# The last three v blocks of a PEER layer, tile by tile, with the norm of each tile behind it

## The chip, the core and the metric

The kernel runs on one core of a Trainium2 chip. The metric is the time of the whole program on the device in microseconds (us), lower is better: 3424.29 us for the kernel before, the median of three runs that gave 3423.9, 3424.29 and 3427.24. A core has a matmul engine (TensorE, called PE in the profile, with its weight loads as PEld), a vector engine (DVE), an activation engine (ACT), GpSimd (POOL), and a queue that issues DMAs (SP). Each engine works through its own instructions in order and waits on semaphores for the others.

## The reference, cut to what matters

The input is 512 tokens of width 1024. There are two residual layers. Each mixes tokens by attention, adds the result to the residual stream `x`, and then adds PEER, a layer of 16384 experts of which every token takes 16 for each of 8 heads:

```python
def rmsnorm(x, g):
    y = xf * lax.rsqrt(jnp.mean(xf * xf, axis=-1, keepdims=True) + NORM_EPS)
    return y * g

    def chunk(args):                       # one chunk of PEER
        h = jax.nn.gelu(jnp.einsum('cd,chkd->chk', xc, u[ec]), approximate=False)
        return jnp.einsum('chk,chkd->cd', gc * h, v[ec])

    for l in range(DEPTH):                 # DEPTH is 2
        ...
        x = x + jnp.concatenate([mix, mo], axis=-1) @ w_out[l]
        x = x + peer(rmsnorm(x, norm_ffn[l]), ...)
        if l == N_A_LAYERS - 1:            # after the first layer
            kv = (rmsnorm(x, shared_norm) @ shared_w_kv)...
    return rmsnorm(x, final_norm)
```

What matters here comes after each PEER: after the first layer the sum of squares of every row of `x`, its root and the normed and turned `x` (features on partitions) for the projections of the second layer; after the second layer the same norm, times the final gain, as the output.

## The kernel before

`x` is kept in SBUF as four tiles of 128 tokens by 1024 features. The program is a row of stages. Each stage has its own buffers and semaphores and ends with a barrier over all engines, so nothing of a later stage starts before the last instruction of the one before has ended.

`peer_stage` (once for each layer) walks over 272 blocks of 128 by 1024 weights: 16 of the query projection, 128 of u, 128 of v. ACT rounds a block to its high part (`hi`, a ring of three), DVE or POOL takes the low part (`lo`), and PE multiplies in three passes: high by high, high by low, low by high. The v blocks multiply the gated hiddens of token tiles 1 to 3, held as `w_hi` and `w_lo` in chunks of four blocks, and add up in six PSUM banks `bank[:, t, half, :]`, where t is 0 to 2 for tiles 1 to 3 and half is one of two halves of 512 features. Token tile 0 is done otherwise: DVE takes its experts' rows one by one and adds them in `acc`. SP loads the blocks, each when the low part four blocks earlier is done.

In `values(n)` PE does all 18 products of one v block and goes to the next. So all six banks are complete only with the last block. Then DVE adds the two `acc` halves to tile 0 (this part comes earlier, while PE works) and adds the banks to tiles 1 to 3, and the stage ends.

After the first layer the stage `turn_stage` ("sht") squares and sums every tile (two on ACT, two on DVE), takes one root for all four, writes four 128 by 128 matrices `diag` with the reciprocal roots on their diagonal, and for each of 8 feature blocks lets PE multiply the four tiles' columns by them, which scales and turns `x` at once. ACT copies the high part out of PSUM and DVE subtracts it for the low part. `value_stage` ("sv") then begins with its weights' DMA. Beside this, SP brings the memory keys and values into SBUF. After the second layer `rstd_stage` ("fin") does all four sums of squares on DVE, and `final_stage` multiplies by the reciprocal root and the gain and stores the tiles.

`out_stage`, earlier in each layer, is not touched. It already works on `x` tile by tile (sum of a half, Square of a half, root, `diag`, turn), with the same kinds of instruction that the change adds, and its functions are cited as "o_" rows.

Of the kernel before, what the change touches and what calls it, by code (L numbers as in the profile page):

```python
# [18 lines left out]
F32 = mybir.dt.float32  # L19
# [67 lines left out]
class Side:  # L87

    def __init__(self, st, pairs):  # L90
        self.pairs = pairs
        self.loaded = [st.sem(f"side{n}") for n in range(len(pairs))]

    def start(self, sp):
        for (dst, src), sem in zip(self.pairs, self.loaded):
            sp.dma_start(dst, src).then_inc(sem, 16)

    def wait(self, sp):
        for sem in self.loaded:
            sp.wait_ge(sem, 16)  # L100

# [25 lines left out]

def rstd_stage(nc, name, src, width, out, side=()):  # L130

    n_src = len(src)
    with Stage(nc, name) as st:
        junk = st.sb("junk", [P, width])
        ssq = st.sb("ssq", [P, n_src])
        squared, meaned, rooted, done = [st.sem(s) for s in ("squared", "meaned", "rooted", "done")]
        side = Side(st, side)
        with nc.Block() as block:
            @block.sync
            def _(sp):  # L140
                side.start(sp)
                side.wait(sp)

            @block.vector
            def _(dve):
                for n in range(n_src):
                    if n:

                        dve.wait_ge(squared, n)
                    dve.tensor_tensor_reduce(junk[:, :], src[n], src[n], 1.0, 0.0, ALU.mult, ALU.add,  # L150
                                             ssq[:, n:n + 1]).then_inc(squared, 1)
                dve.wait_ge(squared, n_src)
                dve.tensor_scalar(ssq[:, :], ssq[:, :], 1.0 / width, EPS, ALU.mult, ALU.add).then_inc(meaned, 1)
                dve.wait_ge(rooted, 1)
                dve.reciprocal(out, ssq[:, :]).then_inc(done, 1)
                dve.wait_ge(done, 1)

            @block.scalar
            def _(act):
                act.wait_ge(meaned, 1)  # L160
                act.activation(ssq[:, :], ssq[:, :], ACT.Sqrt).then_inc(rooted, 1)

def turn_stage(nc, name, ident, parts, out, gain, rstd=None, norm=True, side=()):

    out_hi, out_lo = out
# [2303 lines left out]
```

## Time and profile before

| What | Value |
|---|---|
| Time, median of three runs | 3424.29 us |
| Time of the profiled execution | 3423.7 us |
| Its span (first to last instruction) | 3421.9 us |
| Mean granted PE clock | 0.977 of full speed |
| PE busy | 3255.3 us (95%) |
| DVE busy | 2667.6 us (78%) |
| ACT busy | 1400.2 us (41%) |

### The profile page before, as it was taken

What the parts mean: (1) busy time and instruction counts of PE and PEld (TensorE: products, weight loads), DVE (VectorE), ACT (ScalarE), POOL (GpSimd) and SP (SyncE); (2) the same over time, 40 slices, a digit from 0 to 9 for tenths busy, and PEclk for the clock granted to TensorE, in tenths of its full rate; (3) what the DMA queues carried; (4) which work ended last, traced back from release to release, by engine and by line L of the source; (5) the groups of instructions that cost most, each with busy time, mean ns of one, the idle gap of its engine ahead of it and who ended that gap; (6) DMA issues with size and microseconds to landing.
All of it is one profiled execution on the core that took longest, in us unless ns stands there. A gap on an engine that the chain in (4) does not pass through costs nothing. (4 is left out here: it accounts for less than half of the span.)

```text
span 3421.9 us, 49213 instructions
## 1 busy us (share of the span) xinstructions
PE 3255.3 (95%) x18534; PEld 2913.3 (85%) x18534; DVE 2667.6 (78%) x5415; ACT 1400.2 (41%) x2205; POOL 1098.5 (32%) x666
## 2 busy tenths in 40 slices
PE   7988999999999999998999997999999999999997
PEld 6866899999998888886978876899989998888886
DVE  4664799888976889885367875799898976888886
ACT  3333245544453333333345544235545453333332
POOL 1311363333422465550000001354242422455451
PEclk9998999999999999999999999999999999999999
DMA  4102358878889999994122212348778789999994
GB/s 164 62 7 89 127 163 288 297 268 294 274 310 352 406 392 402 387 397 144 71 80 69 75 44 81 130 138 293 288 268 282 271 313 350 409 398 394 392 396 178
DMA packets 324348, 833.65 MB, mean 244 GB/s; under 512 B 26000, under 2 KB 160656, under 8 KB 320016
## 3 DMA queue, kind: packets, MB, share of 16 engines
q1 hardware_dynamic: 250384, 562.04, 45.8%
q0 software_dynamic: 73728, 268.47, 21.3%
q8 instruction: 148, 2.42, 0.3%
q14 instruction: 88, 0.72, 0.1%
HBM read 721.30 MB, written 109.10 MB: 243 GB/s over the span
## 5 line engine op out<-in xcount | busy, mean ns | idle before, releaser
L1959 ACT ACTIVATE peer_hi<-peer_raw 128x1024 fp32r<-128x1024 f32 x540 | 570.7, 1057 | 648.8 <-PE p_bank L1933 501.1
L2173 DVE TENSOR_TENSOR peer_lo<-peer_raw,peer_hi 128x1024 fp32r<-128x1024 f32 x434 | 532.0, 1226 | 315.2 <-ACT peer_hi L1959 314.9
L1862 POOL DMA_INDIRECT p_grow<-in_u_rows,p_expert x256 | 331.2, 1294 | 750.1 <-DVE p_hid L2181 736.1
L1862 POOL DMA_INDIRECT p_grow<-in_v_rows,p_expert x256 | 425.1, 1660 | 372.4 <-DVE p_acc L2190 331.4
L1933 PE MATMUL p_bank<-peer_hi,p_w_hi 128*128 128x512 f32 x1536 | 473.1, 389 | 0.8 <-DVE peer_lo L2173 0.8
L1933 PE MATMUL p_bank<-peer_hi,p_w_lo 128*128 128x512 f32 x1536 | 473.0, 389 | 0.0
L1933 PE MATMUL p_bank<-peer_lo,p_w_hi 128*128 128x512 f32 x1536 | 472.8, 389 | 0.0
L1884 PE MATMUL p0r_h_ps<-peer_x_hi,peer_hi 128*128 128x384 f32 (+1 forms) x1152 | 400.8, 348 | 9.7 <-ACT p_h_sb L1973 5.8
L1884 PE MATMUL p1r_h_ps<-peer_x_hi,peer_hi 128*128 128x384 f32 (+1 forms) x1152 | 401.1, 348 | 9.3 <-ACT p_h_sb L1973 5.6
L1884 PE MATMUL p1r_h_ps<-peer_x_hi,peer_lo 128*128 128x384 f32 (+1 forms) x1152 | 394.9, 343 | 0.0
L1884 PE MATMUL p1r_h_ps<-peer_x_lo,peer_hi 128*128 128x384 f32 (+1 forms) x1152 | 394.9, 343 | 0.0
L1884 PE MATMUL p0r_h_ps<-peer_x_hi,peer_lo 128*128 128x384 f32 (+1 forms) x1152 | 394.8, 343 | 0.0
L1884 PE MATMUL p0r_h_ps<-peer_x_lo,peer_hi 128*128 128x384 f32 (+1 forms) x1152 | 394.7, 343 | 0.0
L1850 POOL TENSOR_TENSOR peer_lo<-peer_raw,peer_hi 128x1024 fp32r<-128x1024 f32 x106 | 267.9, 2529 | 372.7 <-ACT peer_hi L1959 372.1
L1933 PEld LDWEIGHTS p_bank<-peer_hi,p_w_hi 128*128 128x128 f32 x1536 | 288.1, 188 | 61.4 <-DVE peer_lo L2173 1.7
L1933 PEld LDWEIGHTS p_bank<-peer_hi,p_w_lo 128*128 128x128 f32 x1536 | 288.3, 188 | 60.0
L1933 PEld LDWEIGHTS p_bank<-peer_lo,p_w_hi 128*128 128x128 f32 x1536 | 288.3, 188 | 59.8
L2181 DVE CUSTOM_DVE_ANT_0 p_grow<-p_grow,p_xrow 128x1024 f32<-128x1024 f32 x256 | 318.2, 1248 | 0.8
L2190 DVE SCALAR_TENSOR_TENSOR p_acc<-p_grow,p_w,p_acc 128x1024 f32<-128x1024 f32 x252 | 317.6, 1279 | 0.0
L1884 PEld LDWEIGHTS p0r_h_ps<-peer_x_hi,peer_hi 128*128 128x128 f32 x1152 | 218.5, 190 | 15.3 <-issue 9.1
L1884 PEld LDWEIGHTS p1r_h_ps<-peer_x_hi,peer_hi 128*128 128x128 f32 x1152 | 218.6, 190 | 15.0 <-issue 8.6
L1884 PEld LDWEIGHTS p1r_h_ps<-peer_x_lo,peer_hi 128*128 128x128 f32 x1152 | 218.3, 189 | 5.2
(365 smaller groups left out, 5589.2 us busy)
## 6 DMA issues: line engine op xcount, KB each, us to landing
peer_raw<-in_u SPq DMA_DIRECT2D x256, 512.0 KB, 5.0
peer_raw<-in_v SPq DMA_DIRECT2D x256, 512.0 KB, 9.1
hiddens<-p_h_sb SPq DMA_DIRECT2D x256, 192.0 KB, 3.7
p_w_raw<-hiddens SPq DMA_DIRECT2D x64, 768.0 KB, 8.0
p_g_sb<-gates SPq DMA_DIRECT2D x64, 768.0 KB, 11.7
gates<-x SPq DMA_DIRECT2D x12, 2048.0 KB, 9.6
ba_w<-in_w_b_mix SPq DMA_DIRECT2D x38, 512.0 KB, 3.6
peer_raw<-in_w_peer_q SPq DMA_DIRECT2D x32, 512.0 KB, 3.8
```

Source lines behind the costliest of these rows:

```text
L1850: pool.tensor_tensor(lo[:, m % NH, :], raw[:, m % NR, :], hi[:, m % NH, :].bitcast(F32), ALU.subtract).then_inc(lo_pool, 1)
L1862: pool.indirect_dma_start(out=grow[:, g % RG, :], out_offset=None, in_=table, in_offset=bass.IndirectOffsetOnAxis(ap=expert[:, at:at + 1], ...
L1884: mm = pe.matmul(h_ps[:, n % 2, first:S], a[:, n % NH, at], b[:, k, first:S], start=(k == 0 and s == 0), stop=(k == KC - 1 and s == 2))
L1933: mm = pe.matmul(bank[:, t, half, :], w[:, c % 2, b, t * P:(t + 1) * P], v[:, n % NH, half * HALF:(half + 1) * HALF], start=j == 0 and s = ...
L1959: act.activation(hi[:, n % NH, :], raw[:, n % NR, :], ACT.Copy).then_inc(hi_ready, 1)
L2173: dve.tensor_tensor(lo[:, m % NH, :], raw[:, m % NR, :], hi[:, m % NH, :].bitcast(F32), ALU.subtract).then_inc(lo_dve, 1)
L2181: dve.tensor_tensor_reduce(row, row, xrow[:, :], 1.0, 0.0, ALU.mult, ALU.add, hid0[:, at:at + 1]).then_inc(used, 1)
L2190: dve.scalar_tensor_tensor(out=acc[:, at % 2, :], in0=row, scalar=w0[:, at:at + 1], in1=acc[:, at % 2, :], op0=ALU.mult, op1=ALU.add).then ...
```

## The change

- **v blocks.** The first 125 v blocks go as before. For the last three (`GROUP0` onwards) PE goes over tile and half first and over the blocks inside: nine products for tile 1's first half, nine for its second half, and so on. A half is complete after its nine. The number of products is the same.
- **Tails.** The sum, the norm and the turn (first layer) or the final scaling and the store (second layer) are in `peer_stage`, tile by tile: tile 0, whose sum needs no PE, then 1, 2, 3. ACT does all the Squares, by halves of 512. `turn_x(0)` stands behind the nine products (0,1), `turn_x(1)` behind (2,0), and `turn_x(2)` and `turn_x(3)` behind the last.
- **Stages.** `turn_stage`, `rstd_stage` and `final_stage` are gone. The memory keys and values are loaded in `dilated_stage`, behind its first two weight tiles. The final gain is loaded into `xrow` 40 blocks into the v blocks. The output is stored from `x`.
- **Buffers.** The pair of normed and turned `x` (`h_hi`, `h_lo`) is one buffer for the whole program, where each part had its own.

```diff
@@ peer_stage, SP
+                    if n == FRONT + 40 and final is not None:
+                        sp.wait_ge(used, PAIRS)
+                        sp.dma_start(xrow[:, :], final[0]).then_inc(final_loaded, 16)
+                if final is not None:
+                    for t in range(TT):
+                        sp.wait_ge(scaled, t + 1)
+                        sp.dma_start(final[1][tokens(t), :], x[:, t, :]).then_inc(y_stored[t], 16)
...
@@ peer_stage, PE
-                for n in range(FRONT, BLOCKS):
+                def last_values(t, c, n):
+                    j = n - FRONT
+                    if t == 0 and c == 0:
+                        wait_lo(pe, n)
+                    for s, (w, v) in enumerate(((w_hi, hi), (w_hi, lo), (w_lo, hi))):
+                        mm = pe.matmul(bank[:, t, c, :], w[:, j // CH % 2, j % CH, tokens(t)], v[:, n % NH, half(c)],
+                                       start=False, stop=j == NK - 1 and s == 2)
+                    if n == BLOCKS - 1:
+                        mm.then_inc(halves_done, 1)
+
+                def turn_x(t):
+                    pe.wait_ge(diag_ready, t + 1)
...
+                    for f in range(KC):
+                        if t and f % 4 == 0:
+
+                            pe.wait_ge(x_lo_ready, 2 * (t - 1) + f // 4 + 1)
+                        mm = pe.matmul(turn_ps[:, f // 4, (f % 4) * P:(f % 4 + 1) * P], x[:, t, f * P:(f + 1) * P],
+                                       diag[:, t, :], start=True, stop=True)
+                        if f % 4 == 3:
+                            mm.then_inc(x_turned, 1)
+
+                for n in range(FRONT, GROUP0):
                     values(n)
...
+                for t in range(TD):
+                    for c in range(2):
+                        for n in range(GROUP0, BLOCKS):
+                            last_values(t, c, n)
+                        if final is None and (t, c) in ((0, 1), (2, 0)):
+                            turn_x(t // 2)
+                if final is None:
+                    turn_x(2)
+                    turn_x(3)
@@ peer_stage, ACT
+                for t in range(TT):
+                    for c in range(2):
+                        act.wait_ge(added, x_half_done(t, c))
...
+                        act.activation(junk[:, half(c)], x[:, t, half(c)], ACT.Square,
+                                       accum_out=ssq[:, t, c:c + 1]).then_inc(x_squared, 1)
+                    act.wait_ge(x_meaned, t + 1)
+                    act.activation(ssq[:, t, 1:2], ssq[:, t, 1:2], ACT.Sqrt).then_inc(x_rooted, 1)
+                    if final is None:
+                        for b in range(2):
+                            act.wait_ge(x_turned, 2 * t + b + 1)
+                            act.activation(x_hi[:, 4 * b:4 * b + 4, tokens(t)],
+                                           turn_ps[:, b, :].rearrange("p (f j) -> p f j", j=P),
+                                           ACT.Copy).then_inc(x_hi_ready, 1)
@@ peer_stage, DVE
-                dve.wait_ge(summed, BLOCKS)
-                for t in range(TD):
-                    to = x[:, t + 1, :]
-                    dve.tensor_tensor(to, bank[:, t, :, :].rearrange("p a b -> p (a b)"), to,
-                                      ALU.add).then_inc(added, 1)
-                dve.wait_ge(added, TD + 2)
+                for t in range(TT):
+                    if t:
+                        for c in range(2):
+                            dve.wait_ge(halves_done, 2 * (t - 1) + c + 1)
+                            to = x[:, t, half(c)]
+                            dve.tensor_tensor(to, bank[:, t - 1, c, :], to, ALU.add).then_inc(added, 1)
...
+                    if final is not None:
+                        dve.scalar_tensor_tensor(out=x[:, t, :], in0=x[:, t, :], scalar=rstd[:, t:t + 1],
+                                                 in1=xrow[:, :], op0=ALU.mult, op1=ALU.mult).then_inc(scaled, 1)
+                        continue
+                    dve.tensor_scalar(diag[:, t, :], ident[:, :], rstd[:, t:t + 1], None,
+                                      ALU.mult).then_inc(diag_ready, 1)
+                    for b in range(2):
+                        dve.wait_ge(x_hi_ready, 2 * t + b + 1)
...
@@ dilated_stage, SP
                 load(0)
                 load(1)
+                sp.dma_start(mem_kT[:, :, :], mem_dram[:, 0, :, :]).then_inc(mem_k_loaded, 16)
+                sp.dma_start(mem_v[:, :, :], mem_dram[:, 1, :, :]).then_inc(mem_v_loaded, 16)
```

The two places of which the prediction speaks follow, as the instructions stand in the built programs. The first is DVE at the end of the first layer's PEER. `x<-p_acc,x` is the sum of tile 0, `x<-p_bank,x` that of tiles 1 to 3, `sht_` names belong to the stage that is removed. Before:

```order
L2173 TENSOR_TENSOR peer_lo<-peer_raw,peer_hi 128x1024 x3
L2253 TENSOR_TENSOR x<-p_acc,x 128x1024 x2
L2257 TENSOR_TENSOR x<-p_bank,x 128x1024 x3
L1799 UNCONDITIONAL_BRANCH
L231 UNCONDITIONAL_BRANCH
L239 ISA sht_junk,sht_ssq<-x 128x1024
L239 ISA sht_ssq 128x1
```

And now, to the first row of tile 2:

```order
L2119 TENSOR_TENSOR peer_lo<-peer_raw,peer_hi 128x1024 x3
L2199 TENSOR_TENSOR x<-p_acc,x 128x1024 x2
L2209 TENSOR_SCALAR p_ssq<-p_ssq 128x1
L2213 SCALAR_TENSOR_TENSOR p_ssq<-p_ssq 128x1
L2216 RECIPROCAL rstd<-p_ssq 128x1
L2222 TENSOR_SCALAR p_diag<-ident,rstd 128x128
L2227 TENSOR_TENSOR h_lo<-p_turn_ps,h_hi 128x4x128 x2
L2207 TENSOR_TENSOR x<-p_bank,x 128x512 x2
```

The sum of tile 1 (L2207) stands behind the whole tail of tile 0, and so on for tiles 2 and 3.

The second place is PE at the same time: the end of the nine products (0,1), the turn of tile 0, and the start of the products (1,0). Before, nothing stood between products there.

```order
L1847 MATMUL p_bank<-peer_hi,p_w_hi 128x512
L1847 MATMUL p_bank<-peer_lo,p_w_hi 128x512
L1847 MATMUL p_bank<-peer_hi,p_w_lo 128x512
L1861 MATMUL p_turn_ps<-p_diag,x 128x128 x8
L1847 MATMUL p_bank<-peer_hi,p_w_hi 128x512
L1847 MATMUL p_bank<-peer_lo,p_w_hi 128x512
```

The eight turns have moved from a stage of their own to a place ahead of 36 of the 54 last products.

The third place is DVE at the end of the second layer. There the tail of a tile is the scaling by root and gain:

```order
L2199 TENSOR_TENSOR x<-p_acc,x 128x1024 x2
L2209 TENSOR_SCALAR p_ssq<-p_ssq 128x1
L2213 SCALAR_TENSOR_TENSOR p_ssq<-p_ssq 128x1
L2216 RECIPROCAL rstd<-p_ssq 128x1
L2219 SCALAR_TENSOR_TENSOR x<-x,rstd,p_xrow 128x1024
L2207 TENSOR_TENSOR x<-p_bank,x 128x512 x2
```

The scaling of tile 0, which was the first of four in the last stage, now stands ahead of the sum of tile 1.

## Rows read from the trace of the kernel before

**Rows 1.** The page's first part: busy time and share by engine.

```profile
PE 3255.3 (95%) x18534; PEld 2913.3 (85%) x18534; DVE 2667.6 (78%) x5415; ACT 1400.2 (41%) x2205; POOL 1098.5 (32%) x666
```

**Rows 2.** Windows (start:end, length; PE, PEld, DVE, ACT, POOL; clock; DMA share, GB/s), first boundary.

```profile
1594.00:1602.70 8.70, 0.00 (x0) 0.00 (x0) 6.08 (x11) 3.79 (x6) 0.00 (x0) 0.63 0.19 62
1602.70:1605.00 2.30, 2.28 (x10) 2.28 (x11) 0.56 (x3) 0.17 (x1) 0.00 (x0) 0.50 0.00 0
```

**Rows 3.** Timeline (start, length, engine, line, operation, [idle before]), end of first layer.

```profile
1581.02 0.62 PE L1933 MATMUL p_bank<-peer_hi,p_w_hi 128*128 128x512 f32 x2
1581.28 1.06 ACT L1959 ACTIVATE peer_hi<-peer_raw 128x1024 fp32r<-128x1024 f32 x1 [3.02 <-PE p_bank L1933]
...
1582.37 1.23 DVE L2173 TENSOR_TENSOR peer_lo<-peer_raw,peer_hi 128x1024 fp32r<-128x1024 f32 x1 [2.85 <-ACT peer_hi L1959]
1583.51 2.48 DVE L2253 TENSOR_TENSOR x<-p_acc,x 128x1024 f32<-128x1024 f32 x2
...
1592.80 0.61 PE L1933 MATMUL p_bank<-peer_hi,p_w_lo 128*128 128x512 f32 x2
1593.46 3.49 DVE L2257 TENSOR_TENSOR x<-p_bank,x 128x1024 f32<-128x1024 f32 x3 [7.46 <-PE p_bank L1933]
...
1598.13 1.06 ACT L221 ACTIVATE sht_junk<-x 128x1024 f32<-128x1024 f32 x1 [15.80 <-PEq L126]
...
1612.56 0.69 DVE L252 SCALAR_TENSOR_TENSOR dil_h_lo<-sht_bank,dil_h_hi 128x512 fp32r<-128x512 f32 x1 [0.20 <-ACT dil_h_hi L228]
1614.22 10.55 SPq L282 DMA_DIRECT2D sv_w<-in_w_shared_v  x12
```

**Rows 4.** Timeline, end of second layer and of the program.

```profile
3389.66 0.62 PE L1933 MATMUL p_bank<-peer_hi,p_w_hi 128*128 128x512 f32 x2
...
3392.15 2.48 DVE L2253 TENSOR_TENSOR x<-p_acc,x 128x1024 f32<-128x1024 f32 x2
3402.10 3.49 DVE L2257 TENSOR_TENSOR x<-p_bank,x 128x1024 f32<-128x1024 f32 x3 [7.47 <-PE p_bank L1933]
3406.76 1.28 ACT L161 ACT_TABLE_LOAD   x1 [15.78 <-PEq L126]
3406.84 1.23 DVE L150 CUSTOM_DVE_ANT_0 fin_junk<-x 128x1024 f32<-128x1024 f32 x1 [1.25 <-PEq L126]
...
3413.42 4.88 DVE L2271 SCALAR_TENSOR_TENSOR final_y<-x,rstd,gain_rows 128x1024 f32<-128x1024 f32 x4 [0.89 <-PEq L126]
```

**Rows 5.** Timeline of `out_stage` in the second layer: tile 0, then tile 3.

```profile
2098.96 0.63 ACT L1544 ACTIVATE o_junk<-x 128x512 f32<-128x512 f32 x1 [5.67 <-DVE x L1588]
...
2100.52 1.28 ACT L1547 ACT_TABLE_LOAD   x1
...
2102.25 0.29 DVE L1601 TENSOR_SCALAR o_diag<-ident,rstd 128x128 f32<-128x128 f32 x1
...
2137.07 0.69 DVE L1588 TENSOR_TENSOR x<-o_bank,x 128x512 f32<-128x512 f32 x1 [3.40 <-PE o_bank L1492]
...
2139.60 2.05 PE L1503 MATMUL o_t_ps<-o_diag,x 128*128 128x128 f32 x16 [2.56 <-DVE o_diag L1601]
2140.35 2.18 ACT L1553 ACTIVATE peer_x_hi<-o_t_ps,gains 128x128 fp32r<-128x128 f32 x8 [1.32 <-PE o_t_ps L1503]
```

**Rows 6.** Timeline of `out_stage` in the first layer: the turn of tile 3.

```profile
330.07 3.57 PE L1503 MATMUL o_t_ps<-o_diag,x 128*128 128x128 f32 x16 [2.57 <-DVE o_diag L1601]
```

**Rows 7.** Windows of one microsecond in these two turns.

```profile
330.00:331.00 1.00, 0.93 (x4) 0.93 (x5) 0.02 (x1) 0.00 (x0) 0.00 (x0) 0.50 0.00 0
...
2140.00:2141.00 1.00, 1.00 (x11) 1.00 (x11) 0.00 (x0) 0.65 (x3) 0.00 (x0) 1.00 0.00 0
```

**Rows 8.** Groups by line (count | busy, mean ns | idle before): table loads of the second `out_stage`.

```profile
L1547 ACT ACT_TABLE_LOAD x1 | 1.3, 1283 | 0.0
```

**Rows 9.** Issues of DMAs (queue, count, KB each, median us to landing).

```profile
x<-stream SPq DMA_DIRECT2D x2, 2048.0 KB, 17.2
```

**Rows 10.** Waits of PE (us in total, times, longest) in the second layer's v blocks.

```profile
PE p_bank L1933 <- DVE peer_lo L2173: 0.2, 1, 0.2
```

More of the change, by code:

```diff
@@ L84, in __call__ @@
         self.wait()
[L87 to L100, printed above, removed]
 class Stage:
@@ L127, in __exit__ @@
         self.ctx.close()
[L130 to L161, printed above, removed]
@@ L338, in _, with dilated_stage @@
                         dve.tensor_copy(out(t, c), bank[:, n % 4, 0:cw]).then_inc(moved, 1)
-def dilated_stage(nc, name, ident, ident_b, masks, h, w_dram, gain, rope, v, mem, o, mix_dram):
+def dilated_stage(nc, name, ident, ident_b, masks, h, w_dram, gain, rope, v, mem, mem_dram, o, mix_dram):
     HALF = 2 * P
@@ L1636, with peer_stage @@
 NTD = SD // TB
-def peer_stage(nc, name, ident, iota16, iota2, h, ring, src, x, rstd, rows_of, drams):
+def peer_stage(nc, name, ident, iota16, iota2, h, ring, src, x, rstd, rows_of, drams, final=None):
     BATCH = 8
@@ L2283, in trunk @@
+                if final is None:
+                    dve.wait_ge(x_lo_ready, 2 * TT)
 def trunk(nc, a, out):
@@ L2361, in trunk @@
             with Stage(nc, "dil") as st2:
-                h = pair(st2, "h")
-                turn_stage(nc, "sht", ident, [(x[:, t, :], lambda f: None) for t in range(TT)], h,
-                           lambda f: None, rstd[:, :],
-                           side=[(tile[:, :, :], mem_dram[:, n, :, :]) for n, tile in enumerate(mem)])
                 v = st2.sb("v", [P, TT, NT * P])
@@ L2376, in gain @@
                     return gains[:, which, k:k + 1]
-                dilated_stage(nc, "ba", ident, ident_b, masks, h, a["w_b_mix"], gain, (cos, sin), v, mem, o,
+                dilated_stage(nc, "ba", ident, ident_b, masks, h, a["w_b_mix"], gain, (cos, sin), v, mem, mem_dram, o,
                               mix_dram)
             peer_st = Stage(nc, "peer1")
-            h, ring = peer_buffers(peer_st)
-            mix_out(1, o, True, lambda f: None, h, ring)
-        peer(1, h, ring)
+            ring = peer_ring(peer_st)
+            mix_out(1, o, True, lambda f: None, ring)
+        peer(1, ring, (a["final"].broadcast_to([P, D]), out))
         peer_st.ctx.close()
-        gain_rows = sb("gain_rows", [P, D])
-        rstd_stage(nc, "fin", [x[:, t, :] for t in range(TT)], D, rstd[:, :],
-                   side=[(gain_rows[:, :], a["final"].broadcast_to([P, D]))])
-        final_stage(nc, x, rstd, gain_rows, out)
 def shape_constants():
```

165 lines of the change are left out of this document (56 added, 109 removed).

## The prediction

> **What bounds the kernel now.** I read the page's busy times first: PE is busy 95% of the span [rows 1], so the change, which keeps every product, can only win where PE has nothing to do. Then I took the windows and the timeline around the end of each PEER layer. At the first end PE stands idle for the whole of 1594.00 to 1602.70 and then turns `x` at clock 0.50 [rows 2]. In the timeline the stretch that the change rewrites begins with the first product of the third-last v block, at 1581.02, and ends with the last low part, 1612.56 + 0.69 = 1613.25 [rows 3]. At the second it begins at 3389.66 and ends with the last scaled tile, 3413.42 + 4.88 = 3418.30 [rows 4]. A gain or a loss is a shift of these two ends, 32.2 and 28.6 us after their starts; what follows them (a barrier and the next weights; a store) stays. The reader is to see in the rows which engine ends last in each stretch: DVE, in both.
>
> **Start of the group, same in both layers.** The last v block is rounded by ACT only when the fourth-last is multiplied (1581.28), and its low part is ready at 1582.37 + 1.23 = 1583.60 [rows 3]. Before, PE needed it 36 products later. Now PE needs it after six. A product takes 0.227 us (54 products from 1581.02 to the end of 1592.80 + 0.61, less the overlap of the last) [rows 3], so PE arrives at 1582.38 and waits 1.27 us. Products (0,0) then end at 1584.33 and (0,1) at 1586.37. DVE adds tile 0 at 1583.51 to 1585.99, as before [rows 3].
>
> **Links of a tail.** `out_stage` has run the same chain, so I take its durations [rows 5]. With the table load of the first Sqrt, from the first Square to `diag` is 2102.25 - 2098.96 = 3.29, and PE starts 0.34 later, 3.63 in all. Without it, from the second half's sum to PE is 2139.60 - 2137.07 = 2.53. Two half sums follow each other by about 0.61 (0.69 less an overlap of 0.08; three of 1024 take 3.49 [rows 3]), and the two Squares with their reads are 0.82 apart, which adds 0.21: 3.35 from the first sum to PE. The eight turns take 2.05 at full clock. ACT's copy began 0.75 after the first two of them (0.51 of issue), so 0.24 behind; the second bank's copy is then at 2.29, its low part at about 2.91 to 3.60 after PE's start. The next tile's sum starts 0.07 before that end, so 3.53 after PE's start. Where a tail ends in scaling, it starts where `diag` would (3.01 after the first sum) and takes 1.20 in a row (4.88 for four [rows 4]).
>
> **First layer, at full clock.** Tile 0: Square at 1586.03, PE at 1589.66. PE had nothing since 1586.37, so it stalls 3.3 us in the middle of its products, and 36 products queue behind the waiting turn. Turn to 1591.71, 27 products to 1597.83, then `turn_x(1)`: here DVE is early (sum at 1593.19, `diag` for 1596.5) and PE is the bound. Sum of tile 2 at 1601.36, PE at 1604.71 (its last products ended at 1601.92: idle 2.8). Sum of tile 3 at 1608.24, PE at 1611.59 (idle 4.8), end 1615.19. Before it was 1613.25: **1.9 us later**. The barrier behind it takes 1.18 us at this stage's end (1596.95 to 1598.13) where the removed stage's took 0.97 (1613.25 to 1614.22) [rows 3]: **+0.2**. So in the first layer the overlap costs more than it brings, since DVE runs the tails one after the other and most of them come after the products. The reader can see it in DVE's order: each sum of a bank stands behind the whole tail of the tile ahead.
>
> **Second layer.** No turn, so PE runs through. DVE: Square at 3392.15 + 2.48 + 0.04 = 3394.67, scaling of tile 0 at 3397.96, sum of tile 1 at 3399.16, and then 3.01 + 1.20 = 4.21 for each tile: sums at 3403.37 and 3407.58, last scaling 3410.59 to 3411.87. Before: 3418.30. **6.4 us earlier.** The banks are ready well before (the last about 3403.5). The end of this stage has more semaphores to clear than the final stage had; between nothing and the 0.3 us by which two stage ends already differ I take **+0.2**.
>
> **The clock.** PE's three idle stretches in the first layer (3.3, 2.8, 4.8 us) each stand ahead of a turn. The trace has the same case twice with both outcomes: after 2.57 us of idle one turn ran at clock 0.50 and took 3.57 us, after 2.56 the other at 1.00 and took 2.05 [rows 5 to 7]. So a cold turn costs 1.5 us, and each turn lies on the chain (`turn_x(0)` through PE's queue, 2 and 3 through DVE's). Bounds: 0 and 4.6 for three. The idles here are as long as or longer than the two seen, so I take two of three, **+3.0**.
>
> The Trainium skill speaks against the change here (TensorE: Matmul & The Clock Gate, "HAM oscillation"): bursts of matmuls with waits between them fall back to the low clock and start cold each time. The trace agrees in one of its two cases, at 0.50, and not in the other, at 1.00. By that rule all three turns are cold, which is the second rival below.
>
> **Table load.** Square and Copy cause no load of their own in `out_stage`: one load, of 1.28 us, for four tiles [rows 5, 8]. Before, in the last stage, it lay under DVE's squares (3406.76 [rows 4]); now it is on the chain of tile 0, and is in the 3.29. The skill (ScalarE: Activation LUTs, "What ACT_TABLE_LOAD costs") has some 2.66 us for a switch, with a drain beside the load. By that both layers would end some 1.4 us later, an estimate from that page; the trace shows the root's instruction directly behind the load's 1.28 us, and the sum goes by the trace.
>
> **Cover of what costs nothing.** The gain row (512 KB) joins a stream of loads that fills the DMA engines. The load of `x` in the same blocks is 2048 KB [rows 9], and PE waited 0.2 us in all of the second layer's v blocks [rows 10]: 0, at most 1.3. SP's wait ahead of it is on rows used some 20 blocks earlier. The memory keys and values move behind two weight tiles of `dilated_stage`, and the first scores come two tiles of products later: 0, at most 1. The one home for `h` moves no instruction: 0. The added matmul order in one bank keeps the weight load for each product, as now: 0.
>
> **Sum.** +1.9 + 0.2 - 6.4 + 0.2 + 3.0 = -1.1, on the profiled execution's 3423.7: 3422.6. The median of the runs lies 0.6 above the profiled one (3424.29), so **3423.2 us**.
>
> **Rivals.**
> 1. The clock holds in all three idles. For it: the turn at 2139.60. Against it: the turn at 330.07, with a shorter idle ahead than any here. Then -4.1: 3420.2 us.
> 2. Slower than before: all three turns cold. Place: `turn_x(0)`, `turn_x(2)`, `turn_x(3)` in the first layer. Price 3 x 1.5 = 4.6, and it decides from the point where cold turns cost over 4.1 us, that is, with the third. For it: each idle is over 2.57 us, the last 4.8. Against it: 2139.60. Then +0.5: 3424.8 us; if products near a turn are caught too, some 1.5 more.
> 3. The tails do go under the products. Then only tile 3's tail is exposed: second layer, last half complete at 3403.4, its scaling about 3405.6 to 3406.9, 11.4 saved; first layer, products done at 1600.6, PE 2.5 later, end 1606.8, 6.4 saved. 3406.5 us. Against it: DVE's order, and that the first `diag` needs a chain of over 6 us from the group's start. For it only that PE would be busy all the time in the second layer, which is not where the end is.
> 4. The change does not overlap without cost elsewhere: the gain row holds up the v stream by its full 1.3 us and the memory loads `dilated_stage` by 1. 3425.5 us. The wait of 0.2 us [rows 10] speaks against it.
>
> **How the numbers follow.** Forecast 0.50, rival 1 0.19, rival 2 0.19, rival 3 0.05, rival 4 0.03; the rest, 0.04, is for layouts and stage ends that no row shows, of either sign. What a measurement can tell from no change is about 0.2%, or 6.8 us: faster means below 3417.4, slower above 3431.1. Forecast and rivals 1, 2 and 4 lie inside: same 0.89. Faster is rival 3 and a part of the rest: 0.07. Slower is the rest: 0.04. The range from 3418.8 to 3427.0 holds the first two rivals with the cost bounds of about 1.3 on one side and of 2.3 on the other.
>
> **What would show it.** In the first layer: PE waits for `peer_lo` once, about 1.3 us, in the first group; then for `diag` three times, about 3.3, 2.8 and 4.8 us; the windows at the turns show 0.50 at two of them; the last `h_lo` comes 34 to 39 us after the group's first product, not under 32.2. In the second: scalings 4.2 us apart, the last ending 22.2 us after the group's first product instead of 28.6. The prediction is wrong if the first layer's stretch gets shorter than 32.2 us, if the tails' period is not about 4.2 us, if PE's v blocks lose time elsewhere, or if the table is loaded more than once in a stage's tail.

## The result, and the profile after

The changed kernel takes 3436.11 us (median of 20 runs, 3423.5 to 3440.39), the kernel before, run beside it, 3428.14 us (median of 20, 3422.7 to 3437.19). The ratio is 1.002, with a 95% interval of 1.0013 to 1.0028: slower by 4.5 to 9.6 us. The prediction said 3423.2 us, no change, in a range that ended at 3427.0. It was wrong. (In a later set one run of the kernel before and one of `c1_final_fill` took over 4400 us in a slower state of the chip; the ratios leave both out.)

The profiled execution took 3434.58 us with a span of 3432.8 us, 10.9 us over the span before. First the page: PE is busy 16.2 us longer than before [rows 1], though the trace has the same 18534 matmul records. A busy time that grows with the same work is the first sign of a lower clock.

```profile
PE 3271.5 (95%) x18534; PEld 2922.8 (85%) x18534; DVE 2664.0 (78%) x5429; ACT 1410.7 (41%) x2239; POOL 1087.3 (32%) x666
```

**The first rewritten stretch.** The timeline of the changed kernel at the end of the first layer, which answers to [rows 3]: the group's first product, PE's wait for the last low part, the four turns of `x`, the last low part, the next stage's first load and its first product.

```profile
1581.18 0.39 PE L1847 MATMUL p_bank<-peer_hi,p_w_hi 128*128 128x512 f32 x1
...
1583.68 2.48 DVE L2199 TENSOR_TENSOR x<-p_acc,x 128x1024 f32<-128x1024 f32 x2
...
1583.82 0.50 PE L1847 MATMUL p_bank<-peer_hi,p_w_hi 128*128 128x512 f32 x1 [1.11 <-DVE peer_lo L2119]
...
1589.81 3.55 PE L1861 MATMUL p_turn_ps<-p_diag,x 128*128 128x128 f32 x16 [2.94 <-DVE p_diag L2222]
...
1599.38 1.95 PE L1861 MATMUL p_turn_ps<-p_diag,x 128*128 128x128 f32 x16
...
1605.92 3.16 PE L1861 MATMUL p_turn_ps<-p_diag,x 128*128 128x128 f32 x16 [2.51 <-DVE p_diag L2222]
...
1613.68 3.57 PE L1861 MATMUL p_turn_ps<-p_diag,x 128*128 128x128 f32 x16 [4.60 <-DVE p_diag L2222]
...
1617.91 0.69 DVE L2227 TENSOR_TENSOR h_lo<-p_turn_ps,h_hi 128x512 fp32r<-128x512 f32 x1 [0.80 <-ACT h_hi L1967]
...
1619.88 3.84 SPq L138 DMA_DIRECT2D sv_w<-in_w_shared_v  x8
...
1624.39 0.69 PE L173 MATMUL sv_bank<-sv_w_hi,h_hi 128*128 128x384 f32 x1 [7.14 <-DVE sv_w_lo L181]
```

The stretch lasts from 1581.18 to 1618.60, 37.4 us against 32.2 before [rows 3]: +5.2. The barrier behind it takes 1.28 instead of 0.97: +0.3. The windows inside three of the turns (columns as in [rows 2]) show the clock, where 0.50 is the low level: low in the first and the fourth, low for most of the third, full in the second, which follows 27 products without a wait.

```profile
1590.00:1593.00 3.00, 3.00 (x15) 3.00 (x16) 0.45 (x1) 0.60 (x1) 0.00 (x0) 0.50 0.00 0
1599.50:1601.00 1.50, 1.50 (x16) 1.50 (x15) 0.00 (x0) 0.53 (x1) 0.00 (x0) 1.00 0.00 0
1606.00:1609.00 3.00, 3.00 (x16) 2.79 (x16) 0.69 (x1) 0.60 (x1) 0.00 (x0) 0.61 0.00 0
1614.00:1617.00 3.00, 3.00 (x16) 3.00 (x15) 0.58 (x1) 0.60 (x1) 0.00 (x0) 0.52 0.00 0
```

**The second rewritten stretch.** The end of the program in the changed kernel, which answers to [rows 4]: the group's first product, the table load, the four scalings.

```profile
3406.73 0.39 PE L1847 MATMUL p_bank<-peer_hi,p_w_hi 128*128 128x512 f32 x1
...
3413.30 1.28 ACT L1963 ACT_TABLE_LOAD   x1
...
3415.02 1.28 DVE L2219 SCALAR_TENSOR_TENSOR x<-x,rstd,p_xrow 128x1024 f32<-128x1024 f32 x1
...
3419.22 1.28 DVE L2219 SCALAR_TENSOR_TENSOR x<-x,rstd,p_xrow 128x1024 f32<-128x1024 f32 x1
...
3423.41 1.28 DVE L2219 SCALAR_TENSOR_TENSOR x<-x,rstd,p_xrow 128x1024 f32<-128x1024 f32 x1
...
3427.60 1.28 DVE L2219 SCALAR_TENSOR_TENSOR x<-x,rstd,p_xrow 128x1024 f32<-128x1024 f32 x1
```

It lasts from 3406.73 to 3428.88, 22.15 us against 28.64 [rows 4]: -6.5. From there to the end of the span are 3.9 us against 3.6: +0.3. The two stretches with their ends sum to 5.5 - 6.2 = -0.7 us. The span grew by 10.9. So 11.6 us were lost in stages whose instructions the change does not touch.

**Where they are.** I compared the starts of the same products, stage by stage. The second layer's attention is as long as before up to the last product into `ba_bank` (the query and key projections of `dilated_stage`): the changed kernel gains 0.5 us there. Then come the last attention units of `dilated_stage`, which have no projection between them, and `out_stage`. From the last `ba_bank` product to the first product of the second PEER layer (`p1r_h_ps`) it is 2021.3 to 2144.3 before and 2026.3 to 2162.2 after: 123.0 against 135.9 us, **+12.9**. The second PEER layer up to its rewritten end gives 0.8 back.

Windows over this stretch, its first 50 us and the rest, of the kernel before, and a third up to its last attention unit:

```profile
2021.30:2071.30 50.00, 35.67 (x296) 29.95 (x294) 27.08 (x71) 21.61 (x67) 0.00 (x0) 0.96 0.07 23
2071.30:2144.30 73.00, 59.33 (x289) 49.17 (x289) 36.70 (x70) 33.25 (x72) 9.55 (x4) 0.91 0.25 87
...
2021.30:2067.10 45.80, 35.41 (x296) 29.83 (x294) 23.53 (x60) 21.40 (x66) 0.00 (x0) 1.00 0.08 25
```

and of the changed kernel:

```profile
2026.30:2076.30 50.00, 40.48 (x265) 32.89 (x265) 22.61 (x55) 19.59 (x62) 0.00 (x0) 0.80 0.06 17
2076.30:2162.20 85.90, 66.83 (x322) 55.42 (x321) 41.03 (x86) 35.62 (x78) 9.54 (x4) 0.86 0.22 77
```

In the first 50 us the granted clock is 0.80 instead of 0.96, and PE gets through 265 instructions instead of 296, busy for longer. By these mean clocks PE had the low level for some 44 us of the stretch, against some 17 before. Work that takes 27 us at half the clock takes 13.5 less at full clock, an estimate from the two pairs of rows, and the stretch is 12.9 longer.

The timeline of PE shows how it begins. Before, an attention unit with a wait of 2.40 us for DVE and the one behind it:

```profile
2034.02 1.97 PE L506 MATMUL ba_o_ps<-dil_v,ba_eT 128*128 128x64 f32 x16 [2.40 <-DVE ba_both L649]
...
2035.82 0.59 PE L467 MATMUL ba_s_ps<-masks,ident_b 128*128 128x512 bf16 x2
...
2037.42 1.09 PE L517 MATMUL ba_t_ps<-ident,ba_e 128*128 128x128 f32 x8
...
2039.66 1.97 PE L506 MATMUL ba_o_ps<-dil_v,ba_eT 128*128 128x64 f32 x16 [1.15 <-ACT ba_eT L550]
```

and the same two units in the changed kernel:

```profile
2039.02 2.63 PE L369 MATMUL ba_o_ps<-dil_v,ba_eT 128*128 128x64 f32 x16 [2.39 <-DVE ba_both L512]
...
2041.45 1.06 PE L327 MATMUL ba_s_ps<-masks,ident_b 128*128 128x512 bf16 x2
...
2044.45 1.97 PE L380 MATMUL ba_t_ps<-ident,ba_e 128*128 128x128 f32 x8
...
2047.53 2.00 PE L369 MATMUL ba_o_ps<-dil_v,ba_eT 128*128 128x64 f32 x16 [1.11 <-ACT ba_eT L413]
```

The wait ahead is the same to 0.01 us. Then the same matmuls take 1.06 instead of 0.59 and 1.97 instead of 1.09. The clock did not fall in the wait itself. Windows of the changed kernel, from the wait's end on:

```profile
2039.02:2040.10 1.08, 1.08 (x10) 1.08 (x10) 0.00 (x0) 1.08 (x6) 0.00 (x0) 1.00 0.00 0
2040.10:2047.00 6.90, 6.31 (x30) 4.68 (x29) 1.91 (x4) 0.74 (x3) 0.00 (x0) 0.51 0.01 2
```

PE worked for 1.1 us at the full clock, and then the clock was low for 6.9 us in which PE was busy. In the kernel before it stayed full behind the same wait. The next unit's first product waits for ACT's `ba_eT`, which waits for PE's transposes `ba_t_ps`, so the unit is 2.9 us longer (2039.02 to 2047.53, 8.51 us, against 5.64).

### The profile page after: what moved, and what is told of

Read it like the earlier page. It is cut to its first block and busy times, and to the rows that moved or that the text cites. A ratio compares the mean times of both kernels' runs of the same rounds, so it can differ in the third digit from the quotient of the medians.

```text
span 3432.8 us, 49215 instructions
## 1 busy us (share of the span) xinstructions
PE 3271.5 (95%) x18534; PEld 2922.8 (85%) x18534; DVE 2664.0 (78%) x5429; ACT 1410.7 (41%) x2239; POOL 1087.3 (32%) x666
## 5 line engine op out<-in xcount | busy, mean ns | idle before, releaser
L1756 POOL DMA_INDIRECT p_grow<-in_v_rows,p_expert x256 | 413.6, 1616 | 388.2 <-DVE p_acc L2136 350.2
L1778 PE MATMUL p0r_h_ps<-h_hi,peer_hi 128*128 128x384 f32 (+1 forms) x1152 | 401.1, 348 | 11.3 <-ACT p_h_sb L1903 5.7
L1778 PE MATMUL p1r_h_ps<-h_hi,peer_hi 128*128 128x384 f32 (+1 forms) x1152 | 400.9, 348 | 9.1 <-ACT p_h_sb L1903 5.6
L1778 PE MATMUL p1r_h_ps<-h_hi,peer_lo 128*128 128x384 f32 (+1 forms) x1152 | 394.8, 343 | 0.0
L1778 PE MATMUL p0r_h_ps<-h_lo,peer_hi 128*128 128x384 f32 (+1 forms) x1152 | 394.7, 343 | 0.0
L1778 PE MATMUL p1r_h_ps<-h_lo,peer_hi 128*128 128x384 f32 (+1 forms) x1152 | 394.6, 343 | 0.0
L1778 PE MATMUL p0r_h_ps<-h_hi,peer_lo 128*128 128x384 f32 (+1 forms) x1152 | 394.5, 342 | 0.0
L1778 PEld LDWEIGHTS p0r_h_ps<-h_hi,peer_hi 128*128 128x128 f32 x1152 | 218.4, 190 | 17.4 <-issue 9.2
L1778 PEld LDWEIGHTS p1r_h_ps<-h_hi,peer_hi 128*128 128x128 f32 x1152 | 218.5, 190 | 14.8 <-issue 8.5
L1778 PEld LDWEIGHTS p1r_h_ps<-h_lo,peer_hi 128*128 128x128 f32 x1152 | 218.2, 189 | 5.2
```

Source lines behind the costliest of these rows:

```text
L1756: pool.indirect_dma_start(out=grow[:, g % RG, :], out_offset=None, in_=table, in_offset=bass.IndirectOffsetOnAxis(ap=expert[:, at:at + 1], ...
L1778: mm = pe.matmul(h_ps[:, n % 2, first:S], a[:, n % NH, at], b[:, k, first:S], start=(k == 0 and s == 0), stop=(k == KC - 1 and s == 2))
```

## The experiments

Three theories stood against each other. **A, local:** only the rewritten stretches count, and the low clock in between belongs to the one execution that was profiled. **B, shift:** the change makes what follows start some 5 us later, and untouched stages with waits of PE then lose or keep the clock by where these waits fall. **C, content:** the new `h` buffer or the moved loads of the memory keys and values cause it. Every kernel was run beside the kernel before on the same chip; "stretch" is the time from the last `ba_bank` product to the first of `p1r_h_ps` in its profile.

### Each half of the change alone

`e1_final_only` has the new end of the second layer, and the first layer as before ("plain": v blocks and sums as before, with `turn_stage` behind them):

```
-        peer(0, ring)
+        peer(0, ring, "plain")
```

> The second layer's part alone: the last three v blocks tile by tile and the final norm in peer_stage there, while the first layer keeps the removed turn stage and the old order of v blocks. The one home for h and the loads of the memory keys and values in dilated_stage stay in. Theory A (local: only the two rewritten stretches count, and the some 12 us that the changed kernel's profile loses between 2026 and 2162 in untouched stages are chance of the granted clock): 6.3 us faster than before. Theory B (shift: what follows the first layer's tail starts some 5 us later, and the untouched stages lose clock because of where they now fall in time): also 6.3 us faster, since nothing moves ahead of the second layer's end. Theory C (content: the buffer of h or the moved memory loads slow the dilated and out stages): 2 to 6 us slower than before.

Measured: 3423.32 us against 3424.71, ratio 0.9995 (0.9986 to 1.0004). The interval, -4.8 to +1.4 us, holds neither the -6.3 that A and B expected nor the +2 to +6 of C. The second layer's end has the new scalings 4.2 us apart. The stretch in between took 126.4 us instead of 123.0, which took back half of the 6.5. It began at 2022.0 us, 0.7 later than before, so this loss came without the shift of theory B. It shows in `out_stage` as a low clock with 9 products in 3.5 us, where the kernel before had 1.00 and 17 products in the same place behind its last `ba_bank` product:

```profile
2098.50:2102.00 3.50, 3.50 (x9) 2.72 (x10) 0.49 (x1) 0.00 (x0) 0.00 (x0) 0.52 0.89 289
```

`e2_turn_only` has the new first layer, and the second layer with its final stage as before:

```
-        peer(1, ring, (a["final"]..., out))
+        peer(1, ring, "plain")
+        rstd_stage(nc, "fin", ...)
+        final_stage(nc, x, rstd, gain_rows, out)
```

> The first layer's part alone: tile by tile with norm and turn there, the second layer's end as before (plain order, rstd_stage, final_stage). Theory A (local): the measured stretch of the first layer, 37.4 us against 32.2, so 5.3 us slower than before with the barrier. Theory B (shift) and theory C (content): 5.3 plus the some 9 to 12 us in the untouched stages, 14 to 17 us slower.

Measured: 3445.34 us, ratio 1.0052 (1.0039 to 1.0066), +20.6 us. The rewritten first layer itself explains some 5.5 of it. The stretch in between took 139.6 us, 16.6 more than before. This is more than the 14 to 17 that B and C expected. Against A: the loss is in every run of it (3437.93 at least), not in one execution. Between B and C it decides nothing.

### A delay and nothing else

`e3_before_delay4` is the kernel before, with four multiplies of 128x1024 on DVE, one after the other, ahead of the squares in `turn_stage`. Nothing reads their result.

```
+    for at in range(4):
+        if at:
+            dve.wait_ge(delayed, at)
+        dve.tensor_tensor(junk[:, 0, :], parts[0][0], parts[0][0], ALU.mult).then_inc(delayed, 1)
+    dve.wait_ge(delayed, 4)
     for at, n in enumerate(own_parts):
```

> The kernel before with four extra products of 128x1024 on DVE (some 1.27 us each with their waits) at the start of the turn stage after the first layer: a pure delay of about 5.1 us, the size by which the changed kernel starts its second layer later, and nothing else changed. Theory A (local) and C (content): 5.1 us slower than before. Theory B (shift): 5.1 plus about 9 to 12 us, 14 to 17 us slower, with low clock in the end of the dilated stage and the start of the out stage.

Measured: 3438.2 us, ratio 1.004 (1.0026 to 1.0053), +13.5 us for a delay of 5.00 us (the four multiplies in its timeline). The stretch took 131.7 us, and its windows look like the changed kernel's, with no part of the change in it:

```profile
2025.90:2075.90 50.00, 40.41 (x277) 33.07 (x279) 23.14 (x57) 20.40 (x66) 0.00 (x0) 0.84 0.07 20
2075.90:2157.60 81.70, 63.02 (x304) 52.62 (x304) 40.56 (x84) 34.31 (x73) 9.54 (x4) 0.87 0.23 79
```

It is 0.5 us under the 14 to 17 that B expected, with an interval of 8.9 to 18.2, which leaves out the 5.1 of A and C. This is the run against A and C: a bare delay gives the loss. The added instructions also move the code behind them, and no run tells this from the delay; PE's own instructions are the same.

`e4_after_delay1` is the changed kernel with one such multiply behind the first tile's tail.

> The changed kernel with one extra product of 128x1024 on DVE behind the tail of the first layer: everything after it starts 1.3 us later. Theory A (local): 1.3 us slower than the changed kernel, so about 9 us slower than before as measured, or near 0 if the changed kernel's loss was chance. Theory B (shift): the untouched stages can lose more or less clock; anything from 8 us faster than the changed kernel to 3 us slower, and a different time from run to run only by the clock. Theory C (content): 1.3 us slower than the changed kernel.

Measured: 3430.01 us, ratio 1.002 (1.0011 to 1.0029), which is the changed kernel's own ratio, with 1.25 us more work on its path. Its stretch was 127.4 us and the clock of the first 50 us 0.96, in the profiled execution:

```profile
2030.40:2080.40 50.00, 36.91 (x293) 30.86 (x294) 25.76 (x70) 21.58 (x67) 0.00 (x0) 0.96 0.08 22
```

In this profile more delay cost less. The time does not show it: its interval also holds the changed kernel's ratio with a plain +1.3.

`b1_before_delay2` is as `e3_before_delay4` with two multiplies, 2.48 us.

> Before with two extra DVE operations of 1.28 us ahead of the sums of the first layer's turn: a pure delay of some 2.55 us, nothing else changed. Theories A and C (content): what follows stays as it is, +2.6 us, the stretch from the last `ba_bank` product to the first of `p1r_h_ps` 123 to 124 us. Theory B: the delay does not pass through unchanged; it is half of the 5.1 us whose run lost 8.7 us more in that stretch, so the stretch may take anything from 120 to 132 us and the time is -0.5 to +11.5 us; a value other than +2.6 by over 2 speaks for B, one of +2.6 for neither.

Measured: 3431.73 us against 3427.22, ratio 1.0011 (1.0002 to 1.002). The interval, 0.7 to 6.9 us, holds the bare 2.5: it decides nothing between the theories. Its profile is of use all the same:

```profile
2026.40:2076.40 50.00, 35.65 (x296) 29.95 (x294) 26.52 (x71) 21.62 (x67) 0.00 (x0) 0.96 0.08 23
2076.40:2149.90 73.50, 59.10 (x288) 48.94 (x289) 37.04 (x71) 33.07 (x72) 9.56 (x4) 0.91 0.26 86
```

Its stretch starts 2026.4 us into the span, the changed kernel's 2026.3, and yet the clock stays. So the time since the start of the span does not decide it, and my wording of theory B ("falls some 5 us later") is not a rule from which one could compute. `b2_before_fill`, below, says the same: nothing ahead of its stretch differs from the kernel before, and yet it starts at 2026.5. A shift of 5 us also comes by itself from one execution to the next.

### Filling PE's waits

In the last units of `dilated_stage` PE works about 4.5 us of each 5.65 and waits 1.15 for `ba_eT`. The next kernels have four spare matmuls ahead of each of these units, into a PSUM bank that nothing reads. The whole kernel has 32 of them:

```
+    if first_step(s) == first_step(s + 1):
+        for _ in range(4):
+            pe.matmul(spare[:, :], ident_b[:, :], masks[:, 0, :], start=True, stop=True, ...)
     if 0 <= s - 2 < UNITS:
         output(s - 2)
```

The condition picks the units that have no products of their own.

`a0_after` is the changed kernel again, on the same chip as the three others of this set.

> The changed kernel itself, beside the next three on one chip. In its first profile the untouched stretch between the last product into `ba_bank` and the first into `p1r_h_ps` took 135.9 us against 123.0 before, with the granted clock at 0.50 from 13 us behind the last `ba_bank` product. Theory B (shift: the untouched end of the dilated stage loses its clock because it now falls some 5 us later): the same in this run, 3430 to 3437 us. Theory A (chance: the low clock of that stretch belongs to one execution): in this run it can as well be 123, and the time 3423 to 3427.

> Before with four spare bf16 matmuls of 128x512 on TensorE ahead of each of the units at the end of the dilated stage that have no products of their own, where TensorE waits about 1.15 us in each 5.65 us. They fill those waits with work (nothing reads it). Theory B (the low clock follows these waits where they fall badly, and in the kernel before they fall well, clock 1.00 up to 2064 us): no gain, -1 to +1.5 us, the products may even lie partly on the path. Theory C (the h buffer or the moved loads of memory cause it): likewise nothing. It is the control of the next run.

> The changed kernel with the same four spare matmuls in the same places. Theory B: TensorE has no idle stretch left there, the clock stays at 1.00 through the end of the dilated stage, and the stretch from the last `ba_bank` product to the first of `p1r_h_ps` falls from 135.9 to 123 to 130 us; time 6 to 12 us under the changed kernel's of the same chip. Theory C: the spare products have nothing to do with the cause, the stretch stays at 134 to 138 us and the time within 1.5 us of the changed kernel's.

Measured beside 3427.22 us of the kernel before:

| kernel | us | ratio (95%) | stretch, us |
|---|---|---|---|
| `a0_after` | 3436.59 | 1.0025 (1.0014 to 1.0036) | 137.3 |
| `b2_before_fill` | 3424.99 | 0.9994 (0.9985 to 1.0003) | 123.0 |
| `b3_after_fill` | 3425.75 | 0.9992 (0.9981 to 1.0002) | 126.0 |

The changed kernel's loss and its long stretch came again, which ends theory A. The 32 spare matmuls take 10.8 us off the changed kernel, and their effect on the kernel before is within its interval. The first 50 us of the stretch, `b2_before_fill` first, `b3_after_fill` second:

```profile
2026.50:2076.50 50.00, 42.52 (x328) 32.77 (x326) 27.03 (x70) 21.58 (x67) 0.00 (x0) 0.99 0.08 23
```

```profile
2028.80:2078.80 50.00, 42.57 (x328) 32.82 (x326) 27.03 (x71) 21.58 (x67) 0.00 (x0) 0.99 0.08 22
```

The clock is 0.99 in both and they do the same number of instructions. The waits are shorter, not gone: in `b3_after_fill` the 1.15 us are 0.28 and the 2.4 are 1.5. The changed kernel without them had 265 and 0.80. Theory C has the same `h` buffer and the same moved loads in `b3_after_fill` and cannot explain this.

`c2_delay4_fill` puts the same matmuls into the delayed kernel of before.

> The kernel before with the pure delay of some 5.1 us in the first layer's turn that cost 13.5 us, now with the spare matmuls at the end of the dilated stage. Theory B (the waits of TensorE there turn a delay into a low clock): the delay costs what it lasts, +4 to +7 us, and the stretch from the last `ba_bank` product to the first of `p1r_h_ps` falls from 131.7 to 122 to 127 us. If the excess of the delay has another cause (memory traffic met elsewhere, for instance), +11 to +15 again.

Measured: 3432.22 us against 3426.52, ratio 1.0014 (1.0005 to 1.0023), +5.7 us for 5.00 us of delay, with a stretch of 124.2 us. Without the spare matmuls the same delay cost 13.5, and the intervals of the two (1.7 to 7.9 and 8.9 to 18.2 us) do not meet. The first 50 us:

```profile
2028.30:2078.30 50.00, 42.59 (x328) 32.81 (x326) 27.08 (x71) 21.58 (x67) 0.00 (x0) 1.00 0.08 23
```

### The cold turns, and versions that beat both

`c4_after_fills` is the changed kernel with these matmuls and with spare ones in PE's waits of the first layer's tail, ahead of the turns of tiles 0, 2 and 3:

```
     def turn_x(t):
+        ...
+        for _ in range((11, 0, 9, 16)[t]):
+            pe.matmul(turn_ps[:, 1, :] if t == 0 else bank[:, 0, 0, :], w_hi[...], hi[...],
+                      start=True, stop=True, ...)
         pe.wait_ge(diag_ready, t + 1)
```

Where the cut has "...", the wait for `taken` now stands ahead of the spare matmuls of tile 0, and tiles 2 and 3 first wait for `added`, since their spare matmuls overwrite a bank that DVE adds.

> The changed kernel with both: the spare matmuls at the end of the dilated stage, and 11, 9 and 16 spare 128x512 matmuls in TensorE's three waits of the first layer's tail (2.9, 2.5 and 4.6 us), ahead of the turns of tiles 0, 2 and 3. If those turns are slow (3.2 to 3.6 us instead of 1.95) because TensorE had been idle just before, all four now take 1.95 and the stretch from the sum of the last block's tile 1 to the last low part shrinks by 3 to 5 us; the whole is 3419 to 3424, some 3 to 5 us under the changed kernel with the first fill alone. If they are slow for another reason (fp32 operands, reading x), they stay at 3.2 to 3.6 and the whole stays within 1 us of it.

Measured: 3422.04 us against 3426.52, ratio 0.9982 (0.9973 to 0.999). That is 3.4 us under `b3_after_fill` by the ratios, which come from two sets and have intervals that overlap. The sum of tile 0, the four turns and the last low part in its timeline:

```profile
1585.42 2.48 DVE L2210 TENSOR_TENSOR x<-p_acc,x 128x1024 f32<-128x1024 f32 x2
...
1591.56 2.05 PE L1872 MATMUL p_turn_ps<-p_diag,x 128*128 128x128 f32 x16 [0.45 <-DVE p_diag L2233]
...
1599.62 1.95 PE L1872 MATMUL p_turn_ps<-p_diag,x 128*128 128x128 f32 x16
...
1606.17 2.05 PE L1872 MATMUL p_turn_ps<-p_diag,x 128*128 128x128 f32 x16 [0.47 <-DVE p_diag L2233]
...
1612.82 2.05 PE L1872 MATMUL p_turn_ps<-p_diag,x 128*128 128x128 f32 x16 [0.94 <-DVE p_diag L2233]
...
1615.54 0.69 DVE L2238 TENSOR_TENSOR h_lo<-p_turn_ps,h_hi 128x512 fp32r<-128x512 f32 x1 [0.20 <-ACT h_hi L1978]
```

All take 1.95 to 2.05 us. From the sum of tile 0 (1585.42) to the end of the last low part (1616.23) it is 30.8 us, against 34.9 in the changed kernel (1583.68 to 1618.60) and 29.7 before (1583.51 to 1613.25 [rows 3]). So the cold clock cost 4.1 us of the first stretch, and at full clock the tail by tile still costs 1.1 more than the stage that it replaced, which itself began its turns at the low clock [rows 2].

`c1_final_fill` is `e1_final_only` with the spare matmuls of `dilated_stage`:

> The kernel before with the new end of the program alone (the second layer's tail, as in the run of the final part alone) and the spare matmuls in the waits at the end of the dilated stage. If the second layer's tail is worth the 6.5 us of its own stretch and theory B is right that the rest was eaten by the clock of untouched stages, the gain now comes through: 4 to 8 us under before, 3418 to 3422, with 123 to 126 us from the last `ba_bank` product to the first of `p1r_h_ps`. If the final part alone is worth only the 1.4 us that its own run showed, 3422 to 3425. It is also the version that may beat both kernels.

Measured: 3420.1 us against 3426.52, ratio 0.998 (0.9971 to 0.9989), -6.4 us, with a stretch of 123.2 us. The final part's 6.5 us of its own stretch now show in the time, though up to 2.2 of the 6.4 may be the spare matmuls' own (`b2_before_fill`, an interval that holds zero). This kernel and `c4_after_fills` are both faster than the kernel before by about 0.2%, clear of noise, and their intervals do not part them.

## Why the prediction was wrong

**The steps that held.** PE's wait at the group's start: 1.27 us predicted, 1.11 measured. The first turn of `x` at 1589.66, measured 1589.81. Three idles of 3.3, 2.8 and 4.8 us ahead of turns: 2.94, 2.51 and 4.60. DVE does run the tails one after the other, so rival 3 is out. The second layer: -6.4 predicted, -6.5 measured, with scalings 4.2 us apart. The ends: +0.2 and +0.2 predicted, +0.3 and +0.3 measured. The table load lay on tile 0's chain with its 1.28 us and the root's scalings followed as the sum had them; the longer switch of 2.66 us that the prediction weighed from the Trainium skill (ScalarE: Activation LUTs, "What ACT_TABLE_LOAD costs") did not show.

**A size that was off, with no effect.** Of the three turns I counted two as cold, +3.0 us, and 1.9 for the rest. All three were cold, the third turn for most of its time (3.55, 3.16, 3.57 us), which is rival 2's mechanism, and `c4_after_fills` prices it at 4.1 and the rest at 1.1. Both ways the first stretch loses about 5 us: +4.9 predicted, +5.2 measured. That the two agree is partly luck, since the clock was taken too low (3.0 for 4.1) and the rest too high (1.9 for 1.1). A slip in the chances changed nothing: forecast and rivals 1, 2 and 4 add up to 0.91, and "same" was given 0.89.

**The step that failed** is one sentence at the start: "A gain or a loss is a shift of these two ends [...]; what follows them (a barrier and the next weights; a store) stays." I took what lies between the two ends as rigid, and looked for a low clock only at the turns that the change adds. The terms of the sum come out at -0.7 us where I had -1.1. The 11.6 us that are missing come from what "stays": behind the rewritten stretch lies a row of attention units in which PE waits 1.15 and once 2.4 us, and the first 50 us there ran at a clock of 0.80 instead of 0.96. The runs show in three ways that a delay ahead of these waits can cost more than itself: a bare delay of 5.00 us on the kernel before costs 13.5 us, the same delay with PE's waits filled costs 5.7, and the fill takes 10.8 us off the changed kernel while that of before moves by 2.2, inside its interval.

The rule that the prediction named (the Trainium skill, TensorE: Matmul & The Clock Gate, "HAM oscillation": bursts with waits between them fall back to the low clock) points the right way, and was applied to too small a part of the program. That section's example has waits for DMA of some 3 to 5 us, so it does not by itself foretell a fall behind the shorter waits here. This case's traces agree with it in the changed kernel (clock 0.80 in the first 50 us, with waits of 1.15 and 2.4 us) and not in the kernel before, where the same units ran at 1.00 to their end. That is the point: the same waits can go either way, and the kernel before had them the lucky way. Its profile showed the waits, had I asked. That the full clock of those units was no property of the code shows only with the later runs.

**The range.** It ended at 3427.0, with bounds from the rewritten stretches alone, on a base of 3424.29 from three runs. The kernel before, beside the changed one, gave 3428.14 over 20 runs, so 3.9 of the 12.9 us between 3423.2 and 3436.11 are the base, and the kernel before itself lay outside the range. Against the kernel beside it the change was forecast at -1.1 and measured at +8.0. `e3_before_delay4` shows that a few microseconds of shift can move this kernel by 8.5 us beyond the shift. On the same base a range that holds this would have reached to some 3436, which still just misses 3436.11.

**What stays open.** Which shift is a lucky one. The stretch was 123.0 (before), 123.5 (`b1_before_delay2`), 131.7 (`e3_before_delay4`), 135.9 and 137.3 (the changed kernel twice), 139.6 (`e2_turn_only`) and 127.4 us (`e4_after_delay1`), and no order by the delay explains this series: the changed kernel and `b1_before_delay2` start the stretch within 0.1 us of each other. The profiles do show that the clock first falls in one of three places, counted from the last `ba_bank` product: 13.8 us behind it in the changed kernel, `e2_turn_only` and `e3_before_delay4`; 25.6 behind it in `a0_after` and `e4_after_delay1`; and only some 46 behind it, where the units have ended, in the kernel before, `b1_before_delay2` and `e1_final_only`. In `e3_before_delay4` and then `a0_after`:

```profile
2025.90:2039.70 13.80, 10.20 (x87) 8.58 (x87) 9.74 (x23) 5.81 (x19) 0.00 (x0) 1.00 0.00 1
2039.70:2046.50 6.80, 6.13 (x30) 4.72 (x29) 1.91 (x4) 0.62 (x3) 0.00 (x0) 0.50 0.01 2
```

```profile
2026.00:2051.60 25.60, 19.77 (x169) 16.53 (x167) 13.93 (x34) 11.59 (x38) 0.00 (x0) 1.00 0.08 22
2051.60:2055.00 3.40, 3.40 (x19) 2.17 (x18) 0.00 (x0) 0.23 (x3) 0.00 (x0) 0.51 0.00 0
```

So the changed kernel had two of these places in its two profiles, and shares the first with a kernel that has no part of the change. What picks the place is not shown.

Nor did I settle why the stretch is 126 us in `b3_after_fill` and `c4_after_fills` and 123 in `c1_final_fill`, with the same `h` buffer and moved loads in all three; the difference is in the later part, in `out_stage`, where I filled nothing. The place of the low clock of `e1_final_only` (2098.50 to 2102.00) is low in these two as well, at 0.51, and 1.00 in `c1_final_fill`; why, I do not know. And the profiles are single executions. That the loss is there in the others rests on their times and mean clocks: 18 of the changed kernel's first 20 runs had a mean granted clock of 0.971 to 0.974, and the two at 0.977 were its two fastest (3423.5 and 3428.51 us), while the 21 runs of the kernel before beside `e3_before_delay4` had 0.974 to 0.979.

## What to carry to other kernels

Before a change that shifts a later part of the program is priced, look through that part for stretches in which PE works with waits between, and give each both outcomes of the clock: the difference belongs in the range, even where the change does not touch them. When a change of a few microseconds measures as three times as many, compare the stages that it left alone, with their granted clock, before looking for a cause in the diff. And where such a stretch has a free PSUM bank, spare matmuls in PE's waits, ahead of the instruction that waits, can make its time depend less on where it falls: here the stretch took 123.0 to 139.6 us in the eight profiles without them and 123.0 to 126.3 in the five with them. The new end of the program, 6.5 us shorter in its own stretch, measured -1.4 us without them and -6.4 with them (the spare matmuls alone, with no other change, measured -2.2, inside their interval).

## What the runs showed of the hardware that was not expected

The clock's fall is not a function of the wait alone: behind waits of 2.40 and 2.39 us, in the same place of the same instructions, it stayed full in one execution, and in the other it fell 1.1 us after the wait's end, with PE at work. Yet it is not plain chance from run to run: the changed kernel had its loss in two sets of runs (ratios 1.002 and 1.0025; only 1 of the first 20 was as low as 3423.5 us and one more under 3431), and `e2_turn_only` and `e3_before_delay4` in each of their five runs (at least 3437.93 and 3435.12 us, where the highest of the 21 runs of the kernel before beside them was 3429.73). Nor is the kernel before free of it: in the later sets single runs of it took 3436.51 us at a mean clock of 0.972 and 3435.34 at 0.973.

Once the clock had fallen in such units, PE was busy for more of the time, because the same work was slower: 40.48 of 50 us in the changed kernel against 35.67 before. That did not keep it up: a mean of 0.80 between the levels 1.00 and 0.50 means that it was low for 40% of these 50 us, where before it was for 8%, all of it behind the last unit. The spare matmuls, with 42.5 us busy at mostly full clock, came with 0.99.
